# Where 36 adaptive sums stand among the attention steps of a two-block transformer kernel

## The reference

```python
def mla_attention(q_nope, q_rope, k_nope, k_rope, v):
    ...
        s = jnp.where(kpos[None, :] <= qpos[:, None], s, NEG)
        p = jax.nn.softmax(s, axis=-1).astype(v.dtype)
        return jnp.einsum('bhqk,bkhd->bqhd', p, v)
```

```python
    cond_lat = jax.nn.silu(c)
    cond_ctx = jax.nn.silu(c_ctx)[None, :]
    for i in range(DEPTH_2):
        ...
        m_l = jnp.split(cond_lat @ ada_w[i] + ada_b[i], N_MOD, axis=-1)
        m_c = jnp.split(cond_ctx @ ada_w[i] + ada_b[i], N_MOD, axis=-1)
```

## Time and profile before

| | |
|---|---|
| median of 3 runs | 3813.54 us (3810.05 to 3816.66) |
| the profiled execution, its time | 3804.83 us |
| its span | 3803.0 us |
| granted clock of TensorE, mean | 0.968 |
| TensorE matmuls busy | 3590.0 us, 94% of the span |
| VectorE, ScalarE, GpSimd busy | 1343.6, 1274.3, 1412.6 us |
| DMA | 322.34 MB, 85 GB/s over the span |
| attention of the first layer | 572.8 to 760.0 us of the span |
| attention of the second layer | 1708.5 to 1896.5 us of the span |

### The profile page before, as it was taken

How to read it: one execution, slowest core, us unless ns; L and a number is a source line. 1 busy time by engine, 2 the same in 40 slices (tenths; PEclk the granted TensorE clock), 3 DMA queues, 4 the chain that set the end, 5 groups by cost and what they waited for, 6 DMA issues and landing times. The chain is left out here.

```text
span 3803.0 us, 50702 instructions
## 1 busy us (share of the span) xinstructions
PE 3590.0 (94%) x18374; PEld 2843.3 (75%) x18374; DVE 1343.6 (35%) x1909; ACT 1274.3 (34%) x2005; POOL 1412.6 (37%) x756
## 2 busy tenths in 40 slices
PE   7999899999999999899999996999998997779998
PEld 6888676688887888666688884888886784548886
DVE  4233545552325223545542336111115204561112
ACT  4222434542224223334542224312123234234222
POOL 4444333344444444333344442323222440024443
PEclk8999999999999999999999998999998998989999
DMA  4333343223323333333233332222212322013331
GB/s 132 100 94 88 89 122 112 84 85 98 96 86 101 100 94 90 93 117 107 84 89 100 94 88 67 61 67 61 67 51 60 89 72 66 1 45 89 100 94 61
DMA packets 569026, 322.34 MB, mean 85 GB/s; under 512 B 30266, under 2 KB 563360, under 8 KB 568480
## 3 DMA queue, kind: packets, MB, share of 16 engines
q1 hardware_dynamic: 568864, 320.22, 28.9%
HBM read 318.08 MB, written 2.10 MB: 84 GB/s over the span
## 5 line engine op out<-in xcount | busy, mean ns | idle before, releaser
L859 POOL TENSOR_TENSOR w_lo<-w_raw,w_hi 128x1024 fp32r<-128x1024 f32 x516 | 1270.3, 2462 | 2128.8 <-ACT w_hi L904 2128.7
L904 ACT ACTIVATE w_hi<-w_raw 128x1024 fp32r<-128x1024 f32 x516 | 546.9, 1060 | 1834.7 <-PE psum L2104 1720.4
L2104 PE MATMUL psum<-h_hi,w_hi 128*128 128x512 f32 x1296 | 527.7, 407 | 43.6 <-DVE h_ctx_lo L1496 21.8
L2104 PE MATMUL psum<-xg_hi,w_hi 128*128 128x512 f32 x1408 | 551.9, 392 | 12.1 <-DVE xg_lo L1448 10.3
L2104 PE MATMUL psum<-xg_lo,w_hi 128*128 128x512 f32 x1408 | 549.1, 390 | 0.0
L2104 PE MATMUL psum<-xg_hi,w_lo 128*128 128x512 f32 x1408 | 549.0, 390 | 0.0
L2104 PE MATMUL psum<-h_hi,w_lo 128*128 128x512 f32 x1296 | 512.3, 395 | 0.0
L2104 PE MATMUL psum<-h_lo,w_hi 128*128 128x512 f32 x1296 | 511.9, 395 | 0.0
L2104 PE MATMUL psum<-a_hi,w_hi 128*128 128x512 f32 x1232 | 432.6, 374 | 4.9 <-DVE a_lo L1564 4.2
L2104 PE MATMUL psum<-a_lo,w_hi 128*128 128x512 f32 x1232 | 431.9, 374 | 0.0
L2104 PE MATMUL psum<-a_hi,w_lo 128*128 128x512 f32 x1232 | 431.9, 374 | 0.0
(11 more groups left out here) (423 smaller groups left out, 4327.1 us busy)
## 6 DMA issues: line engine op xcount, KB each, us to landing
w_raw<-ffn_w SPq DMA_DIRECT2D x120, 512.0 KB, 3.8
w_raw<-ffn_w_gate SPq DMA_DIRECT2D x88, 512.0 KB, 3.8
w_raw<-ffn_w_up SPq DMA_DIRECT2D x88, 512.0 KB, 3.8
ada_raw<-ada_w SPq DMA_DIRECT2D x72, 512.0 KB, 4.5
w_raw<-ffn_w_down SPq DMA_DIRECT2D x64, 512.0 KB, 4.1
w_raw<-w_in SPq DMA_DIRECT2D x60, 512.0 KB, 3.8
w_raw<-ffn_w_down SPq DMA_DIRECT2D x32, 384.0 KB, 3.4
w_raw<-w_out SPq DMA_DIRECT2D x24, 512.0 KB, 4.0
```

Of the source, the lines that this page charges most:

```text
L859: nc.gpsimd.tensor_tensor(w_lo[:, i, :], w_raw[:, i, :], w_hi[:, i, :].bitcast(F32), ALU.subtract).then_inc(lo_ready, 1)
L904: nc.scalar.activation(w_hi[:, pos, :], w_raw[:, pos, :], ACT.Copy).then_inc(hi_ready, 1)
L2104: last = nc.tensor.matmul(dst, w[:, pos, k * P:(k + 1) * P], rhs[g][r](k0 + k), start=k == 0 and m == 0, stop=k == nk - 1 and m == 2)
```

## The change

One table of steps is changed. Before, each layer had six adaptive sums in the first tile, three in the second, five in the third and four in the fourth. Now it has ten in the first, none in the second, eight in the third and none in the fourth. There are 18 a layer as before, in the same order, with the same operands; only the step behind which each stands is another, and with it the PSUM bank of a few and the ring buffer that meets a given step.

```diff
-ADA_STEPS = [UN * i + at for i, steps in enumerate(((0, 2, 4, 6, 8, 13), (3, 6, 9), (3, 5, 7, 9, 13), (3, 5, 7, 9))) for at in steps]
+ADA_STEPS = [UN * i + at for i, steps in enumerate(((0, 2, 3, 4, 5, 6, 7, 8, 9, 13), (), (3, 4, 5, 6, 7, 8, 9, 13), ())) for at in steps]
```

## The result

| | before | changed |
|---|---|---|
| median of 8 runs each | 3815.66 us (3810.05 to 3831.34) | 3838.95 us (3833.21 to 3846.76) |
| ratio | | 1.0062, 95% interval 1.0052 to 1.0072 |
| profiled execution, its span | 3804.83, 3803.0 us | 3842.28, 3840.4 us |
| mean granted clock | 0.968 | 0.962 |
| both attentions together, each from its first score matmul to the end of its fourth tile | 375.2 us | 395.9 us |

The kernel became 23 us slower; the forecast was 9.5.

The account below looks back on a forecast made before the run. PE was taken to bound the attention, so waits and clock decide. Per layer 8.6 - 4.8 - 6.4 + 5.5 = 2.9 us, 5.8 for two, plus 3.7 of clock: 3813.54 + 9.5 = 3823.0 us; range 3808 to 3836.

Parts of the forecast that it names:

- Direction and place: Whole kernel slower by 9.5 us; stretches: first tile +9 to +11, second about -5, third +5 to +6, fourth about -6.
- Waits of the first tile: First tile: three new PE waits at steps 3, 4 and 10, 1.0 us each, bounds 0 and 3.0 together.
- Second tile, at full clock: Second tile: three sums and the waits beside them go, 4.8 us less a layer.
- The wait for `h_lo` at step 11: Second tile: PE arrives early at this chain, so of up to 0.98 us freed before it only 0.4 comes back.
- Fourth tile: Fourth tile: four sums and waits at steps 4 and 10 go, 6.4 us less a layer.
- Third tile, waits: Third tile, sum of step 4: new wait for line 1745, 1.0 us second layer, about 0.3 first, 0.7 each taken.
- Loads: Third tile: some loads late by 0.1 to 0.3 us, 0.6 us in the tile, bounds 0 and 2.
- The estimate by the Trainium skill: Two loads would bound every step of 4.0 us, some 2 us in each of six gaps a layer; not adopted.
- The clock: First tile: full clock back about 4 us later, 2 us a layer; third: nothing; 3.7 us taken for both layers.
- the second tile falls to half clock: Second tile: 11 steps of small matmuls at half clock, 9 us a layer more, 3837 us; chance 7%.
- a sign of being wrong: Second tile: the prediction called itself wrong if low clock appears there.
- The rule of the Trainium skill: TensorE: frequent short idles between matmul groups make the clock fall and rise; new idles would cost more than taken.

Follow-up runs that it names:

- a_again: The changed kernel run and traced once more with no edit: 1.0064 of the kernel before.
- g1: The kernel before, no sum moved, with PE made to wait for VectorE at steps 3 and 4 of the first tile: 1.0032.
- g2: The kernel before, with PE made to wait for VectorE ahead of the values of steps 8 and 9 of the first tile: 1.0010.
- h1: The kernel before, with the second tile's three sums moved to steps 5 and 7 of the first and 6 of the third: 1.0016, on another chip 1.0024.
- i1: h1's table, with one score product computed four times more in steps 4, 7 and 10 of the second tile: 1.0047 of the kernel before.
- e2: The kernel before, with the third tile's sums as in the changed kernel and one sum left in the fourth, at step 5: 1.0024.
- f1: The changed kernel, with the sum of step 3 of the first tile moved to step 7 of the second: 1.0045 of the kernel before.

## Why the prediction was right or wrong

- **Direction and place: right in the main.** Slower, and in the first and third tile; but in the three of four traced layers in which the second tile had low clock it gave back only 2.8, 2.8 and 0.5 us.
- **Waits of the first tile: right.** Idle of 0.91 us before line 2461 at step 3, before the values of step 4 and before line 2431 at step 10, where it had 1.0 each. In the low stretch the first two cost the same.
- **Second tile, at full clock: nearly right.** 29.07 us against 33.42 is -4.35, forecast -4.8. The wait for `h_lo` at step 11 was foreseen and is 1.02 us; the 0.52 us for `probs_t` at step 6 was not: PE, with less to do, arrives early at VectorE's copy.

```profile
663.12 0.33 PE L2397 MATMUL psum<-ident,probs 128*128 128x128 f32 x1 [0.52 <-DVE probs_t L1766]
664.02 0.41 PE L2404 MATMUL psum<-ident,cmp_p 128*128 128x128 f32 x2 [0.57 <-ACT probs_t L1158]
...
671.83 0.44 PE L2438 MATMUL psum<-probs_t,v_win 128*64 128x128 f32 x4 [1.02 <-DVE h_lo L1791]
```

- **Fourth tile: right.** -6.0 in each layer, forecast -6.4.
- **Third tile, waits: right.** The new wait is there, 0.94 us in the second layer against 1.0 (in a_again 0.93 in the first). Where low clock lies near it, it is gone or 0.26.

```profile
1841.68 1.07 PE L2461 MATMUL psum<-ada_raw,cond 128*32 128x256 f32 x16 [0.94 <-DVE h_lo L1745]
```

- **Loads: right.** The longest idle of PE for a load in the two traces of the changed kernel is 0.30 us. The landings of the earlier trace rows gave the right price, though single loads took up to 6.7 us. The estimate by the Trainium skill (DMA: Bandwidth & Descriptors, Measured), 2 us in each gap, was not borne out.
- **The clock: wrong, and this is the step that failed.** "I expect it back one round later, about 4 us ... 2 us a layer" for the first tile, and "I take nothing" for the third. In the four layers traced, the first tile's stretch grew by 17, 7, 7 and 7 us, and the second and third tile together by 10.3, 0, 3.4 and 10.2. By busy time the clock cost 15.4 and, in a_again, (65.9 - 42.8) / 2 = 11.6 us, where 3.7 was taken; three of the four first tiles stand at the upper bound that was set (longer by 6.9 us, 3.5 a layer), and the fourth far above it. By tile: the first tiles cost 10.3 and, in a_again, 5.0 us of clock in both layers, where 4 was taken, and the second and third tiles 5.0 and 6.5, where nothing was. So both halves of the term failed: the first tile's was too small, and the other tiles' should not have been zero. For the first tile the runs show what was missed: idle of 1 us twice at steps 3 and 4 goes with long low stretches (g1, and the tally above) and costs more than itself, while at full clock it costs about itself (g2). For the second tile they show that emptying it brings low clock (h1), not by what.
- **The rival "the second tile falls to half clock", 7%, happened in part.** It did not run at half clock throughout (that would have been 9 us a layer), but had 3.4 to 10.2 us of it in three of four traced layers, which the prediction had named as a sign of being wrong, and h1 shows a loss of 0.16 to 0.24% for a table that costs nothing at full clock. Its argument, "it kept 1.00 over the whole tile", was an observation on a tile with three sums in it and said nothing of one without. Its reason, steps of small matmuls only, found no support in i1.
- **The rule of the Trainium skill** (TensorE: Matmul & The Clock Gate, A second HAM failure mode), by which the idles cost more than I took, came out nearer to the runs than my reading. I set it off against one stretch that had no idle in it. But that stretch told only that low clock needs no idle, not that idle does no harm.
- **What the attention does not explain.** The medians differ by 23.3 us, the attentions by 19 to 21. The rest is smaller than what two things behind the attention do from one execution to the next (the last part); it is not shown which.

How idle (g1: 0.32%), an emptied second tile (h1: 0.16 to 0.24%) and the new third and fourth tile (e2: 0.24%) combine to 0.62% was not measured pair by pair; that their sum, 0.7 to 0.8%, is near it is no proof that they add, and f1, without the idle in the low stretch, still loses 0.45%.

## What to carry to other kernels

Where TensorE runs at its lower clock for some microseconds, price idle that a change brings into that stretch by itself: here 4 us of it cost 12 (7 to 18 by the interval), and the same idle in a stretch at full clock cost 4 (0 to 7). A balance of busy time and waits can be right to 2 us in 375 and still miss the result, when a table that moves light work changes how long the clock stays low; two or three traces of each version show how much of that is chance. Moving work from a short tile to a long one takes away what covered the next chain through VectorE and ScalarE there (`probs_t`, `h_lo`).

## What the hardware showed that was not expected

**Two speeds at one granted clock.** The feed-forward part that opens the second block is one run of 3168 matmuls on line 2104, far behind the attention. From the start of its first to the start of its last it took 556.6 to 558.8 us in ten of the seventeen traces and 566.4 to 567.5 in seven. The time at the lower level in it is 3.9 to 8.2 us in both groups, and PE is idle for 3 to 4 us of it. In its middle the granted clock is 1.00 in both. Before, then changed:

```profile
2400.00:2440.00 40.00, 40.00 (x233) 35.00 (x232) 5.60 (x9) 14.19 (x17) 12.04 (x5) 1.00 0.20 59
```
```profile
2440.00:2480.00 40.00, 40.00 (x228) 34.68 (x228) 5.93 (x9) 13.16 (x17) 11.96 (x5) 1.00 0.22 66
```

233 matmuls in 40 us against 228. The changed kernel has both levels (566.9 in its first trace, 557.0 in a_again), so it isn't the change. It is 10 of the 37 us by which the two profiled executions differ (the attentions are 21), and why a profile must not be read by its span alone. Before's runs have groups near 3805 and 3815 us, which fits it, but no trace of before at 3815 was taken. What sets it is open.

**Low clock behind the attention.** Another 6 us of the 37 are clock: from the second attention's end to the end of the kernel PE is busy at the lower level for 98.3 us in the changed kernel's trace and 85.8 in before's. Seven traces have 98.3 to 100.5, ten 84.4 to 90.2. a_again (89.7) and both traces of before are among the ten, and h1's table has one of each (88.0 and 99.2), so the table does not decide it.

**How regular the low stretches of before are.** Its two traced executions have the same four stretches, 44.4 us in each. The two other tables that were traced twice, the changed one and h1's, scattered: 78.5 and 71.7 us, 78.5 and 58.0. Whether before does so near 3815 us was not seen.
